# An expert's next weights issued by SyncE one place later in a routed mixture of experts (one core, FP32)

## The reference, cut to what matters

```python
gates = ...   # top-1 group of 4, then top-2 of the 4 experts in it: 2 experts per token
h = silu(einsum('nd,edf->nef', xt, moe_w1)) * einsum('nd,edf->nef', xt, moe_w3)
y = einsum('nef,efd->nd', h * gates[..., None], moe_w2)
x = layer_norm(ALPHA * x + y, ln2_g, ln2_b)
```

## Time and profile before

| | |
|---|---|
| median of 3 runs | 1230.64 us (1227.58 to 1231.98) |
| the profiled execution: time, span | 1235.21 us, 1233.5 us |
| mean granted TensorE clock | 0.969 of full speed |
| PE busy | 1130.3 us (92% of the span) |
| DVE, ACT, POOL busy | 809.8, 539.6, 183.4 us |
| moved by DMA | 221.06 MB, mean 179 GB/s |
| weight loads by SP | 48 of 1024 KB |
| row loads and stores by SP in the expert part | 41 and 41 of 512 KB |

### The profile page before, as it was taken

One profiled execution on the slowest core, in us unless ns is written; L12 is line 12 of the kernel. 1 busy time (PEld: TensorE's weight loads), 2 busy tenths in 40 slices (PEclk: granted clock), 3 DMA queues, 4 the chain that ended last, 5 costly groups with the idle time before them and its releaser, 6 DMA issues. The chain is left out here.

```text
span 1233.5 us, 20732 instructions
## 1 busy us (share of the span) xinstructions
PE 1130.3 (92%) x5734; PEld 1001.3 (81%) x5735; DVE 809.8 (66%) x1530; ACT 539.6 (44%) x703; POOL 183.4 (15%) x189
## 2 busy tenths in 40 slices
PE   6999999999999999999999893899998999999980
PEld 6999999999999999788888672677887777778760
DVE  4666453464455556577777576665754888788885
ACT  4465343443444445322322223445544665556530
POOL 1000000010000001003332224015001121122222
PEclk9999999999999999999999995999999999999995
DMA  5331597668666534424544216574666778887654
GB/s 190 116 104 63 128 161 91 82 156 104 97 97 222 207 141 161 151 93 162 175 152 137 89 70 245 202 296 169 251 245 256 271 281 318 329 301 262 235 194 166
DMA packets 86987, 221.06 MB, mean 179 GB/s; under 512 B 18992, under 2 KB 45648, under 8 KB 80656
## 3 DMA queue, kind: packets, MB, share of 16 engines
q1 hardware_dynamic: 57824, 129.90, 31.5%
q0 software_dynamic: 18160, 59.53, 14.3%
q10 hardware_dynamic: 10944, 30.95, 13.0%
HBM read 133.75 MB, written 86.58 MB: 179 GB/s over the span
## 5 line engine op out<-in xcount | busy, mean ns | idle before, releaser
L1440 PE MATMUL ps_h<-w_hi,xt_hi 128*128 (+1 forms) x328 | 133.9, 408 | 8.4 <-DVE w_lo L1097 6.2
L1440 PE MATMUL ps_h<-w_hi,xt_lo 128*128 (+1 forms) x328 | 129.3, 394 | 0.0
L1440 PE MATMUL ps_h<-w_lo,xt_hi 128*128 (+1 forms) x328 | 129.3, 394 | 0.0
L287 PE MATMUL ps_vb_c<-x_hi,w_hi 128*128 (+1 forms) x320 | 115.0, 359 | 9.9 <-DVE x_lo L461 9.7
L287 PE MATMUL ps_vb_c<-x_hi,w_lo 128*128 (+1 forms) x320 | 114.4, 358 | 0.0
L287 PE MATMUL ps_vb_c<-x_lo,w_hi 128*128 (+1 forms) x320 | 113.7, 355 | 0.0
L287 PE MATMUL ps_va_b<-x_hi,w_lo 128*128 (+1 forms) x320 | 112.7, 352 | 0.0
L287 PE MATMUL ps_va_b<-x_hi,w_hi 128*128 (+1 forms) x320 | 112.5, 352 | 0.0
L287 PE MATMUL ps_va_b<-x_lo,w_hi 128*128 (+1 forms) x320 | 111.8, 349 | 0.0
L1440 PEld LDWEIGHTS ps_h<-w_hi,xt_hi 128*128 128x128 f32 x328 | 62.6, 191 | 24.8 <-issue 12.6
L1097 DVE TENSOR_TENSOR w_lo<-w_raw,w_hi 128x2048 f32 (+1 forms) x32 | 73.1, 2287 | 6.8 <-ACT w_hi L1092 5.6
(11 more groups left out here) (348 smaller groups left out, 2629.5 us busy)
## 6 DMA issues: line engine op xcount, KB each, us to landing
w_raw<-in_w SPq DMA_DIRECT2D x48, 1024.0 KB
o_scr<-x_raw ACTq DMA_DIRECT2D x42, 512.0 KB, 7.5
w_lo_p<-xs_scr SPq DMA_DIRECT2D x41, 512.0 KB
o_scr<-w_lo_p SPq DMA_DIRECT2D x41, 512.0 KB
w_raw<-in_w_in POOLq DMA_DIRECT2D x19, 512.0 KB, 3.6
xs_scr<-x_raw ACTq DMA_DIRECT2D x17, 512.0 KB, 10.0
x_raw<-in_x_t SPq DMA_DIRECT2D x20, 416.0 KB, 3.5
x_hi_p<-y_scr SPq DMA_DIRECT2D x16, 512.0 KB, 4.2
```

The source lines that it names most:

```text
L287: mm = pe.matmul(ps[i][:, 0:CHUNK], w[:, i, k], x[:, k, bass.ds(c * CHUNK, CHUNK)], start=(k == 0 and n == 0), stop=(k == KT - 1 and n == 2))
L1440: mm = pe.matmul(ps_h[par][:], x[:, par, k], w[:, bass.ds(at, 1), k].rearrange("p o n -> p (o n)"), start=(k == 0 and n == 0), stop=(k == ...
```

## The change

In step s SP no longer asks whether step s is the first of its expert, but whether step s - 1 was, and then issues the weight loads that belonged to step s - 1. Nothing is done in steps 0 and 1 (`early(s, 2)`); the unconditional load of expert 1 ahead of the steps stays.

```diff
@@ SP, step(s, par, h, left, tiles)
                 if left == 3:
                     load_gate(s + 3, 1 - par, h + 1 + par, row)
-                more = sp.value_load(plan[0:1, 3, bass.ds(s, 1)], min_val=0, max_val=1)
-                with sp.If(more):
-                    next_weights(sp, sp.value_load(plan[0:1, 0, bass.ds(s, 1)], min_val=0, max_val=NE - 3) + 2)
+
+                if not early(s, 2):
+                    more = sp.value_load(plan[0:1, 3, bass.ds(s - 1, 1)], min_val=0, max_val=1)
+                    with sp.If(more):
+                        next_weights(sp, sp.value_load(plan[0:1, 0, bass.ds(s - 1, 1)], min_val=0, max_val=NE - 3) + 2)
```

## The result

The changed kernel took 1276.57 us (median of 4 runs, 1273.63 to 1283.45) against 1229.67 us (4 runs) of the kernel before; the ratio is 1.0376, 95% interval 1.034 to 1.0412. The forecast was 1296 us, with a range of 1270 to 1322 us, and slower. The mechanism was right, the size too large: the loss is 46.9 us where 65.7 were summed. The profiled execution took 1283.45 us with a span of 1281.7 us, 48.2 us longer than the one of before, and is the slowest of the four.

What follows compares the result with a forecast made beforehand. PE, busy 92% of the span, was taken as the bound. Terms 65 - 5.6 + 11.3 - 5 = +65.7 us on the profiled 1235.2 gave 1300.9, or 1296 us on the runs' scale; range 1270 to 1322 us.

Steps and rivals of the forecast that it cites:

- Issue one step later: SP's weight loads in the eight two-step distances between experts' first steps: issued later by 70 us together, a mean of 8.75.
- Slack and landing: Weights' DMA in two-step distances: slack covers 3.5 and 1.5 us of the shift; missing a gather saves 5.6 us.
- The clock: PE behind stalls in two-step distances: six new cold stretches at 1.88 us each, +11.3 us.
- Rows and the rest: PE's waits for row loads, 6.6 us in all: rows land sooner when ahead of the weights, -5 us.
- Three steps: Loads used three steps later: the shift is just covered, with 0 to 1.2 us over, so 0 us.
- the signs that were named: ACT waits 7 to 10 us in eight steps; two-step distances 27 to 31 us; mean clock slightly below 0.969.
- faster: Rival: the weights' place is harmless and only rows behind 3 MB of weights gain, 6.6 us, giving 1224 us; chance 0.03.
- no effect: Rival: loads are held at their own waits for DVE's subtraction anyway and move little, 1231 us; chance 0.02.
- small loss: Rival: both halves land in 7 us, no cold stretches, more slack; +28 us, 1258 us; chance 0.08.
- The point named for "faster": What decides it: time from new issue to use exceeds a 9.0 us landing; said to hold with three steps only.

Runs made afterwards that it cites:

- late_from_11: The change applied only to the last three weight loads (experts 11, 12, 13, three steps ahead of the next expert's), against the kernel before: ratio 1.0002.
- after_warm: Changed kernel plus seven extra PE matmuls of 512 columns ahead of the hidden-rows wait, in weight-preparing steps from 7 on: ratio 1.0598 to the kernel before.
- behind_rows: Weight loads one step later as in the change, but behind the row load and ahead of the store, against the kernel before: ratio 1.0004.
- thin_gather: Kernel before with the second gather of a finished tile cut to 64 of 1024 columns, in all tiles but the last three: ratio 0.9966.
- gather_late: Kernel before with POOL's gathers of the paired steps held until PE has finished the step's second layer: ratio 1.0662.

## Why the prediction was right, and where it was too large

- **Issue one step later.** Forecast 70 us over eight distances. Measured from the Silu of the first step to the issue: 67.5 us in all before, 140.5 after, so 73.1 us. The term was right; it includes what the clock did to the path.
- **Slack and landing.** Forecast -5 and -5.6, together -10.6 us. From the issue to the Silu in which the weights are used there were 97.2 us over the eight before and 79.1 after: **-18.1 us**. This is the first mis-sized term. In the distances from 20, 22 and 24 it is -10.0 us where -5.6 were forecast: I had taken 10 us for both halves there, and they land in 8.4 to 8.9 us. In the other five it is -8.1 us where -5 were forecast. I had taken the 9.0 us of step 8 for a landing everywhere, and in the changed kernel both halves are there in 7.5 to 7.6 us in the four early ones. They do not land faster for being late: in late_from_11, where the early loads stand at their old place, they land in 7.3 to 8.2 us. The kernel before had more slack than I gave it, since the trace of it shows when ACT took the weights and not when they landed.
- **The clock.** Forecast +11.3 us, from 1.88 us that a cold second layer cost, taken six times. The path shows about 3: the 73.1 us against the 70 of the shift, and 0.2 to 1.7 us a distance in after_warm. PE's work behind a stall did take 2.4 us more, but part of it lies beside DVE's work. This is the second mis-sized term. The count was off as well: the cold second layer of step 14 begins at 934.10, behind the Silu of step 15, so it lies in the distance from 15 to 18 and not in one of the eight; seven of them were without a cold stretch, not six.
- **Rows and the rest.** Forecast -5 us; the execution outside the eight distances is 6.7 us shorter, and PE's wait for row DMAs fell by 6.1 us. late_from_11 and behind_rows give no gain that the time shows, though, so what made the rest shorter is not shown to be the rows, and that the number came close is luck. Two pieces are something else. The distance from 3 to 6 is 3.8 us shorter (33.6 against 37.4 us), and it lies anywhere between 32.9 and 37.4 us in the traces of kernels that have the same code there (late_from_11, thin_gather and gather_late beside the kernel before). And where the loop ends PE is idle for 4 us in both kernels (in the changed one up to 956.60), and the second layer of step 14 follows it; before, it ran behind the Silu of step 15 and cold, now it runs inside the stall ahead of that Silu, and the distance from 15 to 18 is 27.1 us in place of 31.9. These two pieces are 8.6 us, more than the whole 6.7.
- **Three steps.** Forecast 0; late_from_11 and ACT's rows confirm it.

Together 73.1 - 18.1 = 54.9 for the eight distances (the terms are rounded) and -6.7 for the rest is 48.2 us, the difference of the two spans. The forecast for the same eight was 65 - 5.6 + 11.3 = 70.7; the 15.8 us between are 7.5 of landing and slack and 8.2 of clock. Both terms erred to the high side, so the sum was too high, and the result lies in the lower part of the range.

Of the signs that were named, the first half landed 5.1 to 5.6 us behind its issue, and ACT waited 7.4 to 8.8 us for the two halves in seven of the eight distances (3.6 us from 13 to 15). The distances are 26.2 to 28.6 us, where 27 to 31 were expected, and the mean clock is 0.946.

Of the rivals, "faster" and "no effect" are refuted by the result, and behind_rows says why: the same three loads in the same step, behind the store and ahead of it, are at 1.0376 and 1.0004. The "small loss" rested on landings of 7 us and no cold stretches; the early landings of 7.5 us are near to it, the late ones and the clock are not. The point named for "faster", that the issue must be more than a landing ahead of its use, is what the three-step places show.

## What to carry to other kernels

A DMA that is queued in program order behind an instruction that waits inherits that wait. Ask first which wait stands ahead of a load, not how many transfers do: three loads moved past a row load cost nothing here, moved past a store that waits for the eviction they cost 3.8%, and the same question asked the other way gave a kernel 1.0 to 1.1% faster than the one we began with. And measure a landing time in a stretch where the queue is as full as it will be: a load that leaves a crowded moment lands faster, which pays back part of a delay. Where nobody waits for a load, the start of its user is only an upper bound for its landing.

## What the runs showed of the hardware

While PE stood idle in the stall, the DMA engines were not. The window of the stall in step 22 and the one behind it in the changed kernel (length, busy times, PE first, then PEclk, DMA share, GB/s):

```profile
1037.90:1045.20 7.30, 0.04 (x1) 0.04 (x1) 2.87 (x3) 5.01 (x4) 0.00 (x0) 0.69 1.01 419
1045.20:1054.60 9.40, 9.40 (x35) 7.99 (x36) 8.39 (x9) 6.07 (x8) 0.00 (x0) 0.70 0.41 146
```

In the first window they moved 419 GB/s with a share of 1.01, so all of them were busy and the bytes only started too late. The granted clock was 0.69 and 0.70 of full speed on average in the two windows, each a mix of the levels 1.2 and 2.4 GHz. It fell while PE was idle; behind the stall it was 0.50 up to 1048.0, 0.51 from there to 1051.0, and 1.00 up to 1054.6, while PE was busy all the time.
